# Opening stage of a fused decoder layer: first q, k and v products run over channel pairs, in PSUM banks kept open

## The reference, cut to what matters

```python
mod = (jax.nn.silu(c) @ w_ada[l] + b_ada[l])[:, None, :]     # (B, 1, 6*1024)
sh1, sc1, g1, sh2, sc2, g2 = jnp.split(mod, 6, axis=-1)
h = x * (1.0 + sc1) + sh1
proj = h @ w_in[l]                                           # (B, S, 5376)
q, k, v, pool_in, ga, gb = jnp.split(proj, split_at, axis=-1)
```

## Time and profile before

| | |
|---|---|
| median of 3 runs (2009.01, 2009.21, 2237.9) | 2009.21 us |
| the profiled execution's own time | 2008.32 us |
| its span on core 3 (slowest; the fastest is 2005.7) | 2007.3 us |
| TensorE busy | 1924.0 us, 96% of the span |
| VectorE / ScalarE busy | 887.7 / 783.3 us |
| granted TensorE clock, mean | 0.992 |

### The profile page before, as it was taken

How to read it: one execution, slowest core, us unless ns; L and a number is a source line. 1 busy time by engine, 2 the same in 40 slices (tenths; PEclk the granted TensorE clock), 3 DMA queues, 4 the chain that set the end, 5 groups by cost and what they waited for, 6 DMA issues and landing times.

```text
span 2007.3 us, 33732 instructions; the slowest of 8 cores (2005.7 to 2007.3 us)
## 1 busy us (share of the span) xinstructions
PE 1924.0 (96%) x11888; PEld 1008.2 (50%) x11888; DVE 887.7 (44%) x1442; ACT 783.3 (39%) x1373; POOL 139.8 (7%) x268
## 2 busy tenths in 40 slices
PE   1999999999999999999999999999999999999995
PEld 0666654444446544444455666444444654444444
DVE  0446553552325535525265655355232553552326
ACT  0555442641026326410267544265102642641046
POOL 1100000000000000100000000000000000001000
PEclk9999999999999999999999999999999999999998
DMA  9967553444345735557362125344444483449202
GB/s 195 231 110 127 96 137 64 74 75 82 67 83 102 183 66 114 84 116 164 68 128 42 33 43 137 64 74 69 74 80 81 87 201 64 74 75 162 48 7 79
DMA packets 60115, 193.50 MB, mean 96 GB/s; under 512 B 6960, under 2 KB 9008, under 8 KB 58672
## 3 DMA queue, kind: packets, MB, share of 16 engines
q0 software_dynamic: 38016, 136.20, 40.0%
q1 hardware_dynamic: 21936, 55.14, 9.3%
HBM read 300.24 MB, written 18.87 MB: 159 GB/s over the span
## 4 chain that ended last, share of the span: by engine, by line
PE 92%; DVE 2%; DMA 2%; ACT 2%; issue 2%; POOL 0%; DVEq 0%; ACTq 0%; SPq 0%; POOLq 0%
PE ps L377 82%; PE ps L1046 4%; PE ps L827 3%; PE ps L627 2%; DMA T<-xT 1%; PE ps L599 1%; DMA wring<-w_ada 1%; PE ps L739 1%; DVE T L854 0%; DVE T L613 0%; PE ps L420 0%; ACT sg_t L1007 0%; DVE T L860 0%; ACT T L514 0%; DVE T L1008 0%
## 5 line engine op out<-in xcount | busy, mean ns | idle before, releaser
L377 PE MATMUL ps<-T,wring 128*128 128x512 bf16 (+1 forms) x4672 | 1027.0, 377 | 10.0 <-DVE T L1008 5.6
L377 PEld LDWEIGHTS ps<-T,wring 128*128 128x128 bf16 x4672 | 457.6, 98 | 550.7 <-issue 14.3
L377 PE MATMUL ps<-hT,wring 128*128 128x512 bf16 x1792 | 408.9, 381 | 15.9 <-ACT hT L473 13.3
L1007 ACT ACTIVATE sg_t<-ps 128x512 f32<-128x512 f32 x176 | 103.1, 596 | 531.3 <-PE ps L377 524.6
L1008 DVE TENSOR_TENSOR T<-ps,sg_t 128x512 bf16<-128x512 f32 x176 | 120.3, 691 | 418.0 <-PE ps L377 364.7
L961 DVE SCALAR_TENSOR_TENSOR T<-ps,GA,T 128x512 f32<-128x512 f32 (+1 forms) x264 | 193.8, 734 | 215.5 <-PE ps L377 210.3
L377 PEld LDWEIGHTS ps<-hT,wring 128*128 128x128 bf16 x1792 | 172.2, 98 | 221.5 <-issue 24.3
L377 PE MATMUL ps<-wring,hT 128*128 128x256 bf16 x1856 | 212.6, 276 | 0.5 <-ACT u_t L512 0.3
L377 PEld LDWEIGHTS ps<-wring,hT 128*128 128x128 bf16 x1856 | 189.0, 107 | 23.5 <-issue 1.3
L618 ACT ACTIVATE T<-T 128x256 bf16<-128x256 f32 (+1 forms) x232 | 109.0, 478 | 110.9 <-DVE T L613 97.7
L815 ACT CAST ybs_t<-T 128x512 bf16<-128x512 f32 (+1 forms) x136 | 80.3, 590 | 104.4 <-DVE T L961 104.3
(11 more groups left out here) (84 smaller groups left out, 1128.0 us busy)
## 6 DMA issues: line engine op xcount, KB each, us to landing
wring<-w_gate POOLq DMA_DIRECT2D x40, 512.0 KB, 6.1
wring<-w_up POOLq DMA_DIRECT2D x40, 512.0 KB, 7.1
T<-xT SPq DMA_DIRECT2D x32, 512.0 KB, 10.1
wring<-w_down POOLq DMA_DIRECT2D x32, 512.0 KB, 7.0
T<-xT SPq DMA_DIRECT2D x14, 1024.0 KB, 11.1
outT<-T SPq DMA_DIRECT2D x56, 256.0 KB, 5.6
wring<-w_ada POOLq DMA_DIRECT2D x24, 512.0 KB, 12.5
wring<-w_pi POOLq DMA_DIRECT2D x16, 512.0 KB, 5.8
```

Of the source, the lines that this page charges most:

```text
L377: fns = [lambda lhsT=lhsT, rhs=rhs, i=i: nc.tensor.matmul(psum[bank][:, cols[0]:cols[1]], lhsT, rhs, start=(i == 0), stop=(i == n - 1)) fo ...
L1007: k.op(ACT, lambda: nc.scalar.activation(sg_t[:, si, :], psum[bg][:, :], AF.Silu), reads=[ps_reg[bg]], writes=[r_sg[si]])
```

## The change

The order of the opening is changed. x of the first two quarters (1024 tokens) is loaded by pairs of channel chunks, 1 MB in one request each (`load_pair`). For each pair i the two `mod_unit`s that belong to it run, `hT` of both quarters is made for its two chunks, and `oq(i)` adds the part of these two chunks to the products: q and k of both quarters, and v of the first. Their 6 PSUM banks stay open (held) over the four pairs; two banks are left for the `mod_unit`s. After the fourth pair `ov` evacuates the six. v of the second quarter and the last two quarters of tokens follow as before, each with its `mod`s written ahead of its first product. The blocks `w_qk[0]` and `w_v[0]` move to places 3 and 4 of the weight order.

```diff
+            def load_pair(i, after):
+                rds = [] if k.dry else [ring["landed"][after]]
+                k.dma(SP, tl_x[i], [(aT1.A(i * 2048, [[1024, 2], [1, 1024]]),
+                                     xT[0].rearrange("(k p) t -> p k t", p=P)[:, 2 * i:2 * i + 2, 0:1024])],
+                      reads=rds, writes=aT1.R(i * 2048, 2048))
...
+        def opening_units():
+            st = {}
+
+            def mms(bk, c0, n, pairs, first, last, final):
+                k.group([lambda lh=lh, rh=rh, kk=kk: nc.tensor.matmul(psum[bk][:, c0:c0 + n], lh, rh, start=(kk == 0 and first), stop=(kk == KC - 1 and last))
+                         for (kk, lh, rh) in pairs], reads=st["rd"], writes=[ps_reg[bk]], inc=final)
+
+            def oq(i):
+                if i == 0:
+                    st["s"] = wload(wfull(w_qk[0]))
+                    st["v"] = wload(wfull(w_v[0]))
+                    st["b"] = [new_bank(hold=True) for _ in range(6)]
...
+                kks = (2 * i, 2 * i + 1)
+                for tt in range(2):
+                    st["rd"] = [r_w[sl]] + [r_hT[kk][tt] for kk in kks]
+                    for mc in range(2):
+                        mms(st["b"][2 * tt + mc], 0, 512, [(kk, wv(sl, kk, mc * 128, 128), hT[:, kk, tt * 512:(tt + 1) * 512]) for kk in kks], True, True, i == 3)
+                st["rd"] = [r_w[sv]] + [r_hT[kk][0] for kk in kks]
+                for gb in range(4):
+                    for kk in kks:
+                        mms(st["b"][4 + gb // 2], (gb % 2) * 256, 256, [(kk, hT[:, kk, gb * 128:gb * 128 + 128], wv(sv, kk, 0, 256))],
+                            gb % 2 == 0, gb % 2 == 1, i == 3 and kk == KC - 1)
+
+            def ov():
+                for bk in st["b"]:
+                    ps_held[bk] = False
...
@@ def seq_body
-                for i in range(2):
-                    for it in pairs[i]:
-                        mod_unit(it)
-                    emit_derived1(i)
-                for tt, after in enumerate((3, 7, 8, 9)):
-                    load(tt, after)
+                for i in range(4):
+                    if i == 0:
+                        pump()
+                        load_pair(0, 0)
+                    mod_unit(pairs[i][0])
+                    if i < 3:
+                        load_pair(i + 1, (2, 5, 7)[i])
+                    mod_unit(pairs[i][1])
+                    emit_derived1(i)
+                    for m in (2 * i, 2 * i + 1):
+                        for tt in range(2):
+                            mod(tt, m)
+                    oq(i)
+                load(2, 9)
+                load(3, 9)
                 emit_consts1()
-                for i in range(2, 4):
-                    for it in pairs[i]:
-                        mod_unit(it)
-                    emit_derived1(i)
-                    for m in (range(0, 4) if i == 2 else range(4, 8)):
-                        mod(0, m)
                 emit_consts2()
-                qk, vv = qk_units(0), v_units(0)
-                for tt in range(4):
-                    for i in range(2):
-                        qk[2 * tt + i]()
-                        if tt < 3:
-                            for m in range(4 * i, 4 * i + 4):
-                                mod(tt + 1, m)
+                ov()
+                for f in vv[2:4]:
+                    f()
+                for tt in range(2, 4):
+                    for m in range(KC):
+                        mod(tt, m)
+                    run(qk[2 * tt:2 * tt + 2])
                     run(vv[2 * tt:2 * tt + 2])
```

More of the change, by code:

```diff
@@ L459, in load @@
                 regs = [r_ for m in range(KC) for r_ in stage(tt, m)[1]]
-                if tt < 2:
-                    dsts = [aT1.A(tt * 4096 + hh * 2048, [[512, 4], [1, 512]]) for hh in range(2)]
-                elif tt == 2:
+                if tt == 2:
                     dsts = [aT4.A(hh * 2048, [[512, 4], [1, 512]]) for hh in range(2)]
@@ L477, in mod @@
                         dst, src, sc(A1, m, 0), sc(modT, m, 0), ALU.mult, ALU.add), reads=regs + [r_mp[m // 2]], writes=[r_hT[m][tt]])
-            return load, mod
+            return load_pair, load, mod
         def s0_early(b):
@@ L519, in copy_evac, with qk_units @@
                     k.op(DVE, lambda: nc.vector.tensor_scalar(dst, src, scl, None, ALU.mult), reads=rds, writes=wrs)
[L521 removed]
+        opening_slots = []
+        def qk_units(ph, eng=None, st=None):
             g, hp = divmod(ph, 2)
             base = (ph % 2) * 4096
[L524 removed]
+            st = {} if st is None else st
             units = []
@@ L528, in u @@
                     def u(mc=mc, tt=tt):
-                        if mc == 0 and tt == 0:
+                        if "s" not in st:
                             st["s"] = wload(wfull(w_qk[ph]), [r_xg] if ph == 1 else ())
@@ L549, in qk_units, with v_units @@
             return units
-        def v_units(g, eng=None):
-            st = {}
+        def v_units(g, eng=None, st=None):
+            st = {} if st is None else st
             units = []
@@ L555, in u @@
                 def u(pr=pr):
-                    if pr == 0:
-                        st["s"] = wload(wfull(w_v[g]))
-                    sv = st["s"]
+                    if "v" not in st:
+                        st["v"] = wload(wfull(w_v[g]))
+                    sv = st["v"]
                     gb = 2 * pr
@@ L570, in v_units @@
             return units
+        def opening_units():
[8 more added lines that the diff above has]
+                    st["b"] = [new_bank(hold=True) for _ in range(6)]
+                sl, sv = st["s"], st["v"]
+                kks = (2 * i, 2 * i + 1)
[12 more added lines that the diff above has]
+                for tt in range(2):
+                    for mc in range(2):
+                        bk = st["b"][2 * tt + mc]
+                        copy_evac(k.evac_eng(), aT2.A(mc * 2048 + 512 * tt, [[1, 512]]), psum[bk][:, :], 0.125 if mc == 0 else None,
+                                  [ps_reg[bk]], aT2.R(mc * 2048 + 512 * tt, 512))
+                for j in range(2):
+                    bk = st["b"][4 + j]
+                    copy_evac(k.evac_eng(), aT3.A(j * 512, [[1, 512]]), psum[bk][:, :], None, [ps_reg[bk]], aT3.R(j * 512, 512))
+            opening_slots.append(st)
+            return oq, ov
         def pt_ap(sidx, rel, dims):
@@ L1167, in seq_body @@
             if b == 0:
-                load, mod = s0_first()
+                load_pair, load, mod = s0_first()
                 pairs = ((4, 0), (5, 1), (6, 2), (7, 3))
-                for i in range(2):
-                    for it in pairs[i]:
-                        mod_unit(it)
-                    emit_derived1(i)
-                for tt, after in enumerate((3, 7, 8, 9)):
-                    load(tt, after)
-                emit_consts1()
-                for i in range(2, 4):
-                    for it in pairs[i]:
-                        mod_unit(it)
-                    emit_derived1(i)
-                    for m in (range(0, 4) if i == 2 else range(4, 8)):
-                        mod(0, m)
-                emit_consts2()
-                qk, vv = qk_units(0), v_units(0)
-                for tt in range(4):
-                    for i in range(2):
-                        qk[2 * tt + i]()
-                        if tt < 3:
-                            for m in range(4 * i, 4 * i + 4):
-                                mod(tt + 1, m)
+                oq, ov = opening_units()
+                ost = opening_slots.pop()
+                qk, vv = qk_units(0, None, ost), v_units(0, None, ost)
+                for i in range(4):
[6 more added lines that the diff above has]
+                    mod_unit(pairs[i][1])
+                    emit_derived1(i)
+                    for m in (2 * i, 2 * i + 1):
+                        for tt in range(2):
+                            mod(tt, m)
+                    oq(i)
+                load(2, 9)
+                load(3, 9)
+                emit_consts1()
+                emit_consts2()
+                ov()
[5 more added lines that the diff above has]
+                    run(qk[2 * tt:2 * tt + 2])
                     run(vv[2 * tt:2 * tt + 2])
```

2 lines of the change are left out of this document (1 added, 1 removed).

## The result

The change is slower: three runs of it took 2035.16, 2035.66 and 2036.61 us, the kernel before 2009.01 and 2009.21. The ratio is 1.0134, with a 95% interval of 1.0120 to 1.0148, so about 27 us, inside the 2% that count as no change. The forecast was +20 and a range up to 2034; the time lies 2 us above the range. (Runs in which a group of cores ran at a visibly lower clock are left out; beside experiments 7, 8, 11 and 12 most runs of the kernel before took about 2035 for that reason, so no ratio is used there and the lowest times are compared, 2008.61 for before.)

A forecast was written before the change was run, and what follows sets the result against it. TensorE was taken as full except in the opening, which transfers bound. Third quarter at 75.7, plus 3.3, 9.31, 3.0 and 7.0, put first scores at 98.3 instead of 78.3: +20.0, so 2029 us, range 2021 to 2034.

The forecast's parts named there:

- the gate: Weight queue: `w_qk[1]` and blocks behind it no longer wait for x, putting 18.1 us of weight bytes ahead of x.
- The added wait on blocks 11 and 12: SP's request for the last quarter of x waits for these blocks, in by 60 us; covered by the third quarter's transfer.
- the gap: TensorE before the last quarter: its `mod`s stand behind the third quarter's last v evacuation, costing 3.0 us.
- one mixed stream: Opening transfers: ten weight blocks and four channel pairs take 44.3 us from 7.05, the last pair landing at 51.4.
- the sum for the third quarter: x of the third quarter shares with 18.1 us of weights, takes 24.3 us and lands at 75.7.
- rival 1: Queues take turns of equal bytes, so the third quarter lands at 70.3: +14.6, 2024 us; chance 0.08.
- the slow restart: TensorE after the 3 us gap before the last quarter: bounds no cost and 2.4 us, none taken.
- 2: Weights don't hold x back; x lands at 57.8 and 64.2: +4.3, 2013 us; chance 0.12.
- 3: Not slower: x goes ahead of the weights and runs faster, third quarter in by 58.3: -1.5, 2007.7 us; chance 0.04.
- 4: Slower by over 2% (40 us), the moved opening meeting a stretch of lower granted clock; chance 0.02.
- 5: Loss partly won back later, weights lying ready when attention starts; at most 0.5 us of idle TensorE: 2026 to 2028; chance 0.04.

The follow-up runs named there:

- experiment 7: Kernel before with x of the first two quarters requested by channel pair, as in experiment 5, but pairing chunks i and i + 4: 2022.37 us in a single run.
- experiment 8: Changed kernel, gate still missing, with the first 4 MB of x in four requests of four chunks by 512 tokens: median 2035.97 us, lowest 2033.46.
- experiment 11: Changed kernel with gate put back, third and last quarters' `mod`s moved, `mod_unit`s one pair ahead, third quarter of x requested one block earlier: median 2012.38 us, lowest 2011.78.
- experiment 12: As experiment 11, but the first 4 MB of x come in requests of four chunks instead of pairs: lowest 2012.42 us.
- experiment 1: Changed kernel with the gate put back, no weight block beyond the tenth requested before the last quarter of x is: 2018.37 us, ratio 1.0049.
- experiment 2: Kernel before with only the gate taken away, so `w_qk[1]` and the blocks behind it no longer wait for x: 2026.10 us, ratio 1.0085.
- experiment 3: Changed kernel with the `mod`s of the last quarter moved between the q/k groups of the third: 2033.05 us, ratio 1.0120.
- experiment 5: Kernel before with x of the first two quarters in four channel-pair requests, two after the fourth block, two after the eighth: 2016.25 us, ratio 1.0034.
- experiment 4: As experiment 1, but each channel pair comes in two requests of 512 tokens, rows of 2 KB: 2022.37 us, ratio 1.0067.
- experiment 6: Kernel before with the first quarter of x requested after the first weight block, not the fourth: 2009.44 us, ratio 1.0001.

## Why the prediction was right and wrong

**Right: the gate.** The term that decided, 18.1 us of weight bytes ahead of x, is confirmed from both sides: 17.5 come back when the gate is put back (experiment 1), and 17 are lost when it alone is taken away (experiment 2). The added wait on blocks 11 and 12 let SP ask for the last quarter at 64.75 (60 in the forecast), while the third quarter was under way until 81.5: covered as said.

**Right: the gap.** 2.77 for 3.0, from 94.4 to 97.14, and experiment 3 shows that VectorE's order makes it. From the start of the third quarter to that of the last 12.39 passed; the forecast had 12.3. What TensorE does between the fourth pair and its wait took 9.1 us (61.3 to 70.4) instead of 11.3; that is hidden under the wait for x and changes nothing.

**Wrong: "one mixed stream [that] lasts 10 x 3.15 + 4 x 3.2 = 44.3", with the fourth pair in at 51.4 and the third quarter at 75.7.** Measured: 61.3 (ScalarE's first `mod` of the pair starts at 61.29) and 81.5. This is the step that failed: the price of the stream, taken from rows with requests of four chunks. Two things are in the first number. 14.7 MB were to have been read by then; it was 16.4 MB, since `w_qk[1]`, a piece of the `w_ada` block behind it and half a MB of the third quarter had come between. At the 332 GB/s of the forecast these 1.7 MB are 5.1 us, but they mostly change places with the fourth pair, and the sum for the third quarter contained them. The rest is the rate: 16.4 MB take 49.4 us at 332 GB/s and took 54.3 at 302.

Up to 81.5 it was 23.3 MB at 313 GB/s, which is 4.3 us more than at 332. The other 1.5 of the +5.8 are bytes: 23.3 MB instead of 22.8, since 1.2 MB that stand behind the third quarter on SP's queue were read before it was whole, and 0.7 MB of weights had been read before 7 us. On core 0, at 335 GB/s, the third quarter was in at 74.8. The text said that the sum held "as long as the engines don't idle". They did not (share 1.01), but each transfer took longer (a weight transfer 0.39 us of an engine's time from 20 to 25 us, 0.32 in the earlier trace rows), so a busy share was the wrong thing to lean on.

What the low rate hangs on: on the two-chunk requests. It comes with them in either order of work (after, experiment 5), with 2 KB and 4 KB rows (experiment 4), with near and far chunks (experiment 7), though a core or two out of step often escape it; it stays away with requests of four chunks, in the old order early or late (before, experiment 6), in the new one (experiment 12 against 11, where nothing else differs), and with an ungated weight queue (experiment 2). The Trainium skill ("DMA: Bandwidth & Descriptors", section "Queues, rings and completion order") says that an engine drains a packet of some 9 to 17 descriptors from one queue before it switches. The counts of this case, 182 to 184 and 116 to 116, do not tell how long a turn is, only that the turns come out equal in transfers whether x has 2 KB or 4 KB in one. That x gets equal transfers and not equal bytes refutes rival 1, as the forecast expected.

**Mis-sized: the slow restart, "I take none".** The last quarter took 8.49 instead of 7.0 on the slowest core. The bounds were 0 and 2.4, and it measured 1.5. It isn't the gap alone: behind the same 2.77 five of the eight cores took 5.07 to 5.26 for the first 16 matmuls, three took 3.61. What differs is the granted clock. Core 6 behind its gap, then core 0 behind its own, which ended at 89.22:

```profile
97.00:100.00 3.00, 2.86 (x7) 1.05 (x8) 0.00 (x0) 0.00 (x0) 0.00 (x0) 0.50 0.91 328
```

```profile
89.00:92.00 3.00, 2.78 (x13) 1.30 (x14) 0.08 (x1) 0.60 (x1) 0.00 (x0) 1.00 0.87 314
```

On the five it fell to 0.50 (1.2 GHz) in the last half microsecond of the gap; on the three it stayed at 1.00. The slow start at 48.10 before looks the same in pace (16 matmuls in 5.98; in 6.12 at 84.75, at a clock of 0.50), though the profile gives 1.00 there; no run shows why. Since the slowest core sets the time, the worse case should have been taken. So 98.3 + 5.8 + 1.5 = 105.6.

**Rivals.** 2 and 3 needed x of the third quarter by 57.8 and 58.3; it was in at 81.5. 4 (over 2%) did not come, at 1.34%. 5 (won back later) didn't either: +27.3 at the scores, +27.3 at the end.

**Is there a version that gains?** None was found. With gate, gaps and order repaired it comes to 2012 (experiments 11 and 12), 3 above before. The early products run in pieces with `mod_unit`s and waits between them, and what TensorE gains by its earlier start it loses there (experiment 12: 35.6 for 30.2). The full rate of bytes brought nothing there: experiments 11 and 12 differ in it and hardly in time, though whole requests also make the second half of `oq(0)` wait for its x until 45.52.

**Open.** Why two-chunk requests are slow. Seven cores fall and rise together and go up to 410 GB/s in between, which speaks for something that cores share and that evens out only in part; no run isolates it. What the rate alone is worth in the total of the kernel after is not measured either, since experiment 8 made a second hole; core 0 (96.3 where the slowest has 105.6) is the nearest to it. Of those 9.4, part is the clock behind the gaps.

## What to carry to other kernels

When steps change their order in a program, look for the waits that they carried for others: here a read of x kept 18 us of weights behind it, and the step that set that wait moved behind its readers. Price a stream of bytes by rows with the same shape of request, and read the rate, not the busy share. And before products are cut into pieces to start early, follow who stands behind each piece in its engine's order: here the engine that waited for x also freed the slots for weights.

## What the runs showed of the hardware

- Two queues on the same engines share nearly one transfer to one, whatever their sizes: 182 to 184 (4 KB and 2 KB written), 116 to 116 (4 KB and 4 KB), 189 to 190. From 65 to 70 us of the kernel after the weights were ahead on two cores (183 to 162, 194 to 156).
- A request's number of chunks sets its rate beside weights. Mean read from 7 to 48 us with requests of four chunks: 327 to 335 GB/s before, 329 to 332 in experiment 12. With two chunks: 305 to 311 on seven cores of the kernel after, 305 to 317 on six in experiment 11, with 240 to 290 and 378 to 410 in single stretches of 4 us; a core out of step can keep 324 to 332. Alone, pairs went at 210 GB/s with the engines 103% busy (experiment 5, core 3), a quarter at 338 with 102.5%.
- A gap of 2.77 us in TensorE was followed by 5.07 to 5.26 us for 16 matmuls on the five cores whose granted clock fell to 0.50 at its end, and by 3.61 on the three where it stayed at 1.00.
